# Input fetched transposed in four pieces with the first weights, its squares summed in PSUM, and two weight slices multiplied in native fp32

## The chip, the cores and the metric

The kernel runs on one core of a Trainium2 chip. The metric is the device time of one execution in microseconds (us). Before the change the median of three runs is 904.51 us (904.27 to 905.12).

The engines have these names: PE is TensorE (PEld its weight loads), DVE is VectorE, ACT is ScalarE, POOL is GpSimd, SP is the engine that issues most transfers.

## The reference

One layer on 256 tokens of 1024 channels: a norm, an input projection, three mixers side by side, an output projection with a residual, and a product-key expert layer over 16384 experts.

```python
h = rms_norm(x, norm1_g)              # x: (1, 256, 1024)
proj = h @ w_in                       # 2816 columns
ua, qb, kb, vb, qc, kc, vc, gc = jnp.split(proj, SPLIT_POINTS, axis=-1)
ya = rms_unit(s5_mixer(ua, ...))      # 256 columns: state space, complex phases, a scan over tokens
yb = rms_unit(moba_mixer(qb, kb, vb, ...))            # 8 heads of 64; here one causal block of 256
yc = retention_mixer(qc, kc, vc, gc, ...)             # 4 heads of 64
x = x + (concat(ya, yb, yc) * mix_out_g) @ w_out
x = x + peer_layer(rms_norm(x, norm2_g), w_q, sub_keys, u_emb, v_emb)
```

In `rms_norm` every token is divided by the root of its mean square plus 1e-6 and every channel is multiplied by its gain.

## The kernel before

**Numbers.** Most matmuls are done in halves: an fp32 operand is split into a high part of type fp32r (ScalarE's copy, `w_hi` or `h_hi`) and the rest (`w_lo` or `h_lo`, a subtraction on GpSimd or VectorE). A product of two such operands is three fp32r matmuls, high by high, high by low, low by high (`halves_product`, L438). A native fp32 matmul needs no halves.

**Input projection.** `w_in` comes in six chunks: the s5 input `u` (256 columns, `w_src[0]`) and five of 512 columns, numbered 1 to 5 (q, k and so on). Each chunk lies in one of three slots of `w_ring`, and is cut into eight slices of 128 rows. Slice m (0 to 39) is row block m % 8 of chunk 1 + m // 8. For slice m ScalarE writes `w_hi[:, m % 4]` (`slices_high`, L1399), GpSimd `w_lo[:, m % 4]` (`slices_low`, L1767), and TensorE does six matmuls of 512 columns, three for each half of the tokens (`by_slices`, L464), accumulating over the eight slices in PSUM. The four places of `w_hi` and `w_lo` are used again as `half_used` counts TensorE's slices.

**The front.** The input is loaded by rows into `xs` in two halves of the tokens (L344). TensorE runs eight warming matmuls on zeros (L449), then transposes the input into PSUM banks 0 to 3 (L419). ScalarE squares both halves of the input with the sum over the row as a by-product (L1428). The gained transposed input `hT` (eight chunks of 128 channels by 256 tokens) is written by ScalarE (chunks 0 to 3, `full`, L1459) and VectorE (4 to 7, L892). Chunk `u` is multiplied in native fp32 from `hT` (L459), without the norm's factor; that factor, `rx`, comes from the root on ScalarE (L1397) and a reciprocal on VectorE (L832) and is applied per token when results leave PSUM. The input's high halves are written by ScalarE (0 to 5, `rounded`) and GpSimd (6, 7), the low ones by GpSimd and, for 4 and 5, VectorE.

**The s5 part.** VectorE computes the decay and angle of each state from the parameters (L850 to L878). Phases come from `phase_turns` (a product of time and rate, then two passes that take the whole turns away) and ScalarE's Sin passes `phase_sines`, `phase_sizes`, `phase_cosines`. The second half of the states has its turns from ScalarE (`second_turns`, `second_rounded_up`) and one VectorE pass (L1043), which counts `turn_ready` to 2. TensorE transposes `u` (L519) and the input matrices `bb` (L525), and multiplies them in four drives (`drive(0)` to `drive(3)`, L434). After each drive VectorE runs the complex states (`states(n)`, L986: products, four scans, products).

**What sets the order.** The program is written out by hand, one instruction stream per engine, each strictly in its written order, joined by semaphores. TensorE's order around the change (L515 to L566) interleaves slices with the transposes and drives:

```python
by_slices(1, range(3, KC))
by_slices(2, range(0, 4))
pe.wait_ge(turn_ready, S5_C)      # the second half's turns
drive(1)
by_slices(2, range(4, KC))
turn_heads(0)                     # needs the rotated q of VectorE
by_slices(3, range(0, 6))
pe.wait_ge(states_ready, 2)
drive(2)
```

SP issues the loads in the order of L342 to L366. A slot's next chunk waits until `lo_ready`, GpSimd's count of low halves, shows that the slot is free. The residual is read from `xs` at L1171, after the output projection.

After the projection come the attention and retention scores, the output projection, the queries, and then 128 tiles of expert keys and 128 of values, which fill most of the span; the change touches only their counts on `lo_ready` and `hi_ready`.

## Time and profile before

| | |
|---|---|
| median of 3 runs | 904.51 us |
| profiled execution, its own time | 903.81 us |
| its span | 901.9 us |
| PE busy | 895.0 us (99%) |
| PE weight loads | 780.3 us (87%) |
| DVE busy | 728.9 us (81%) |
| ACT busy | 565.5 us (63%) |
| POOL busy | 426.7 us (47%) |
| DMA | 191.52 MB, mean 212 GB/s |

A row of a timeline gives the start in the span and the duration in us, the line of the code, the operation with what it writes and reads, and in brackets how long the engine was idle before it and what ended that. Matmuls overlap, so the step from one start to the next says more than a matmul's own duration. A native fp32 matmul is recorded as two matmuls.

### The profile page before, as it was taken

The numbers are of one execution on the slowest core, as the hardware profiler recorded it, in microseconds if no ns is written. First come the engines' busy times: TensorE is split into PE (matmuls) and PEld (weight loads), VectorE is DVE, ScalarE is ACT, GpSimd is POOL, SyncE is SP. The second block draws the span as 40 slices with busy tenths as digits, with TensorE's granted clock in tenths as the row PEclk, the third lists the DMA queues.
The fourth block names the chain that finished last, engine by engine and source line by source line (L and its number), as shares of the span: only waits on it lengthen the run. The fifth ranks groups of instructions, "written<-read, shape, count | busy, mean of one in ns | idle before, by whom it ended". The sixth has DMA issues, their size and how long they took to land.

```text
span 901.9 us, 18888 instructions
## 1 busy us (share of the span) xinstructions
PE 895.0 (99%) x5158; PEld 780.3 (87%) x5158; DVE 728.9 (81%) x1659; ACT 565.5 (63%) x1144; POOL 426.7 (47%) x342
## 2 busy tenths in 40 slices
PE   8999999999999999999999999999999999999998
PEld 7777888999999998888888898888888888888886
DVE  7979545299997449999999987888888888888886
ACT  7759566655444567777777776656565655656563
POOL 5875288888888987777777773000000000000000
PEclk9999999999999999999999999999999999999999
DMA  9825050556666665655465557676676766666663
GB/s 337 299 103 187 1 210 24 203 208 231 232 224 224 216 233 188 219 186 218 182 221 183 211 196 258 239 245 237 235 245 242 243 242 243 236 235 247 241 242 128
DMA packets 67755, 191.52 MB, mean 212 GB/s; under 512 B 6672, under 2 KB 8592, under 8 KB 67728
## 3 DMA queue, kind: packets, MB, share of 16 engines
q1 hardware_dynamic: 67440, 191.09, 59.9%
q8 instruction: 14, 0.23, 0.1%
q10 hardware_dynamic: 288, 0.10, 0.0%
q14 instruction: 13, 0.11, 0.0%
HBM read 173.86 MB, written 17.30 MB: 212 GB/s over the span
## 4 chain that ended last, share of the span: by engine, by line
PE 94%; DVE 3%; DMA 1%; ACT 1%; SPq 0%; issue 0%; POOL 0%; DVEq 0%
PE ps L442 20%; PE ps L444 20%; PE ps L443 20%; PE ps L754 16%; PE ps L756 7%; PE ps L764 3%; PE ps L708 1%; PE ps L753 1%; DMA routing<-in_w_in 1%; DVE ps L827 1%; DVE routing L827 1%; PE ps L710 1%; DVE ps L1005 1%; PE ps L727 0%; PE ps L602 0%; PE ps L434 0%
## 5 line engine op out<-in xcount | busy, mean ns | idle before, releaser
L1644 ACT ACTIVATE w_hi<-raw 128x512 fp32r<-128x512 f32 x512 | 308.3, 628 | 135.9 <-PE ps L444 135.1
L1810 POOL TENSOR_TENSOR w_lo<-raw,w_hi 128x512 fp32r<-128x512 f32 x256 | 327.3, 1300 | 69.3 <-ACT w_hi L1644 68.9
L754 PE MATMUL ps<-h_both,w_hi 128*128 128x512 f32 x632 | 225.8, 393 | 0.0
L827 DVE TENSOR_TENSOR w_lo<-raw,w_hi 128x512 fp32r<-128x512 f32 x256 | 177.4, 693 | 57.1 <-ACT w_hi L1644 42.2
L442 PE MATMUL ps<-w_hi,hot_gate 128*128 128x512 f32 x512 | 199.2, 389 | 0.0
L443 PE MATMUL ps<-w_lo,hot_gate 128*128 128x512 f32 x512 | 199.2, 389 | 0.0
L444 PE MATMUL ps<-w_hi,hot_gate 128*128 128x512 f32 x512 | 199.2, 389 | 0.0
L756 PE MATMUL ps<-h_both,w_lo 128*128 128x256 f32 x553 | 154.9, 280 | 0.0
L754 PEld LDWEIGHTS ps<-h_both,w_hi 128*128 128x128 f32 x632 | 117.9, 187 | 20.4
L444 PEld LDWEIGHTS ps<-w_hi,hot_gate 128*128 128x128 f32 x512 | 96.1, 188 | 20.1
L443 PEld LDWEIGHTS ps<-w_lo,hot_gate 128*128 128x128 f32 x512 | 96.1, 188 | 20.0
L442 PEld LDWEIGHTS ps<-w_hi,hot_gate 128*128 128x128 f32 x512 | 96.1, 188 | 19.8
L442 PE MATMUL ps<-h_both,w_hi 128*128 128x256 f32 x392 | 111.1, 284 | 0.0
L1775 POOL TENSOR_TENSOR w_lo<-routing,w_hi 128x512 fp32r<-128x512 f32 x72 | 91.9, 1298 | 40.5 <-ACT w_hi L1411 39.5
L443 PE MATMUL ps<-h_both,w_hi 128*128 128x256 f32 x392 | 110.9, 283 | 0.0
L444 PE MATMUL ps<-h_both,w_lo 128*128 128x256 f32 x392 | 110.9, 283 | 0.0
L1326 DVE SCALAR_TENSOR_TENSOR hot_gate<-ps,route_t 128x256 fp32r<-128x256 f32 x256 | 105.7, 475 | 0.0
L756 PEld LDWEIGHTS ps<-h_both,w_lo 128*128 128x128 f32 x553 | 104.4, 189 | 0.4
L1673 ACT ACTIVATE acts<-ps 128x256 f32<-128x256 f32 x128 | 49.1, 383 | 74.1 <-PE ps L444 66.3
L827 DVE TENSOR_TENSOR route_t<-acts,routing 128x256 f32<-128x256 f32 x128 | 81.6, 637 | 2.5 <-ACT acts L1673 2.0
L443 PEld LDWEIGHTS ps<-h_both,w_hi 128*128 128x128 f32 x392 | 75.2, 192 | 0.2
L442 PEld LDWEIGHTS ps<-h_both,w_hi 128*128 128x128 f32 x392 | 75.2, 192 | 0.1
(242 smaller groups left out, 1236.0 us busy)
## 6 DMA issues: line engine op xcount, KB each, us to landing
raw<-in_u_t SPq DMA_DIRECT2D x128, 512.0 KB, 3.4
raw<-in_v SPq DMA_DIRECT2D x128, 512.0 KB, 3.2
act_spill<-acts SPq DMA_DIRECT2D x62, 256.0 KB, 2.2
acts<-act_spill SPq DMA_DIRECT2D x62, 256.0 KB, 3.4
routing<-in_w_in SPq DMA_DIRECT2D x4, 2048.0 KB, 13.3
routing<-in_w_out SPq DMA_DIRECT2D x2, 2048.0 KB, 8.3
routing<-in_w_q SPq DMA_DIRECT2D x2, 2048.0 KB, 7.6
routing<-in_w_in SPq DMA_DIRECT2D x2, 1024.0 KB, 10.2
```

Source lines behind the costliest of these rows:

```text
L442: pe.matmul(dst, s_hi, m_hi, start=first and i == 0, stop=False)
L443: pe.matmul(dst, s_hi, m_lo, start=False, stop=False)
L444: mm = pe.matmul(dst, s_lo, m_hi, start=False, stop=end)
L754: mm = pe.matmul(ps[:, s % 2, :], s_hi, both, start=(h == 0 and k == 0), stop=end)
L756: mm = pe.matmul(ps[:, s % 2, 0:S], s_lo, m_hi, start=False, stop=False)
L764: mm = pe.matmul(ps[:, 4 + 2 * (s % 2) + q // 2, (q % 2) * 2 * NKEY:(q % 2 + 1) * 2 * NKEY], hot_j[:, s % 2, q, :], hot_gate[:, s % 2, q]. ...
L827: return V.tensor_tensor(out_, a, b, op)
L1326: ins = V.scalar_tensor_tensor(hot_gate[:, s % 2, q], iota_p.unsqueeze(1).to_broadcast([P, 2, NKEY]), route_t[:, 0, one], route_t[:, 2:4, ...
L1644: A.activation(w_hi[:, 2 * (s % 2) + h, :], raw[:, s, h * HALF:(h + 1) * HALF], ACT.Copy)\
L1673: A.activation(acts[:, s, :], ps[:, s % 2, 0:S], ACT.Gelu_apprx_tanh).then_inc(act_ready, 1)
L1775: G.tensor_tensor(w_lo[:, m % 4, :], w_ring[n % W_SLOTS][:, k, :], w_hi[:, m % 4, :].bitcast(F32), ALU.subtract).then_inc(lo_ready, 1)
L1810: G.tensor_tensor(w_lo[:, slot, :], raw[:, s, h * HALF:(h + 1) * HALF], w_hi[:, slot, :].bitcast(F32), ALU.subtract).then_inc(lo_ready, 1)
```

## The change

- The input is also given transposed (`x_t`), and the `u` weights in an order in which a partition's rows lie together (`w_u`). SP loads both in four pieces each, in turn: two chunks of channels of the input (256 KB), two of the weights (256 KB). `xT` lies where the rotation's scratch lies later. The input by rows is loaded later, ahead of the wait for chunk 6 of the weights.
- The transposes of the input go; the warming matmuls are 13 and not 8. The first product waits for a piece of weights every two chunks.
- `hT` is made from `xT` in SBUF, chunks 0 to 3 by ScalarE, 4 to 7 by GpSimd.
- ScalarE squares the four pieces, 512 columns each, the first into PSUM bank 2; VectorE adds them there (five additions), and TensorE sums over the partitions with two one-column fp32 matmuls with a column of ones. ScalarE's root reads that PSUM column.
- Slices 0 and 1 are multiplied in native fp32 from `hT` and the weights; they have no halves, so the counts of `lo_ready` and `hi_ready` are two lower throughout.
- The order on each engine changes: on TensorE the transposes of `u` come after slice 3, those of `bb` after slice 5, the first drive after slice 6, the second after slice 13. On ScalarE the root follows high half 2, and the Sin table the copies of `u`. On VectorE the reciprocal stands inside `phase_turns`, and the low halves of input chunks 0 and 1 after `bb`. On GpSimd the input's halves lie between the slices' low halves.

```diff
+NATIVE = 2
+        xT = rot_tmp.rearrange("p (k t) -> p k t", k=KC)
+        x_sq = qk_flat.rearrange("p (i n) -> p i n", i=4)
+        x_ss, x_part = mv[:, 1, 0:S], mv[:, 1, S:2 * S]
...
             sp.dma_start(vec[:], vecs).then_inc(params_in, 16)
-            for t in range(TT):
-                sp.dma_start(xs[:, t, :], x[t * P:(t + 1) * P, :]).then_inc(x_in[t], 16)
-            first = w_src[0].rearrange("(k p) n -> p k n", p=P)
-            sp.dma_start(w_ring[0][:, 0:4, 0:S5_CH], first[:, 0:4]).then_inc(first_in, 16)
-            sp.dma_start(w_ring[0][:, 4:KC, 0:S5_CH], first[:, 4:KC]).then_inc(w_in_sem[0], 16)
+            for i in range(4):
+                ks = slice(2 * i, 2 * i + 2)
+                sp.dma_start(xT[:, ks], x_t[:, ks]).then_inc(x_t_in[i], 16)
+                sp.dma_start(w_ring[0][:, ks, 0:S5_CH], w_u[:, ks]).then_inc(first_in[i] if i < 3 else w_in_sem[0], 16)
...
                 elif 3 < n <= 8:
-                    sp.wait_ge(lo_ready, KC * (n - W_SLOTS))
+                    if n == 6:
+                        for t in range(TT):
+                            sp.dma_start(xs[:, t, :], x[t * P:(t + 1) * P, :]).then_inc(x_in[t], 16)
+                    sp.wait_ge(lo_ready, KC * (n - W_SLOTS) - NATIVE)
...
-            keep_warm(mv[:, 0, 0:P], 7, 8)
-            pe.wait_ge(con_in, 16)
-            transpose_rows(xs, x_in)
+            keep_warm(mv[:, 0, 0:P], 7, 13)
             for k in range(KC):
-                if k == 0:
-                    pe.wait_ge(first_in, 16)
-                if k == 4:
-                    pe.wait_ge(w_in_sem[0], 16)
-                pe.wait_ge(full_act if k < 4 else full_dve, k % 4 + 1)
+                if k % 2 == 0:
+                    pe.wait_ge(first_in[k // 2] if k < 6 else w_in_sem[0], 16)
+                pe.wait_ge(full_act if k < 4 else full_pool, k % 4 + 1)
...
+            pe.wait_ge(zeros_ready, 6)
+            pe.wait_ge(ss_ready, 1)
+            for t in range(TT):
+                mm = pe.matmul(ps[:, 5, t:t + 1], x_ss[:, t * P:(t + 1) * P], ones, start=True, stop=True)
+            mm.then_inc(ss_psum, 1)
+
+            def native_slices(ks):
+
+                pe.wait_ge(second_in, 16)
+                for k in ks:
+                    for t in range(TT):
+                        mm = pe.matmul(ps[:, t, :], hT[:, k, t * P:(t + 1) * P], w_ring[1][:, k, :], start=(k == 0), stop=False)
+                    mm.then_inc(half_used, 1)
...
-            by_slices(1, range(0, 1))
+            native_slices(range(NATIVE))
+            by_slices(1, range(2, 4))
+            pe.wait_ge(con_in, 16)
             pe.wait_ge(u_tok_ready, TT)
...
-            by_slices(1, range(1, 2))
+            by_slices(1, range(4, 6))
             pe.wait_ge(bb_ready, 1)
...
-            by_slices(1, range(2, 3))
+            by_slices(1, range(6, 7))
             pe.wait_ge(u_ready, 1)
             pe.wait_ge(bT_ready, 1)
             drive(0)
-            by_slices(1, range(3, KC))
-            by_slices(2, range(0, 4))
+            by_slices(1, range(7, KC))
+            by_slices(2, range(0, 6))
             pe.wait_ge(turn_ready, S5_C)
             drive(1)
-            by_slices(2, range(4, KC))
+            by_slices(2, range(6, KC))
...
-            dve.wait_ge(sumsq_x, TT)
-            for k in range(4, KC):
-                dve.wait_ge(t_psum, k // 2 + 1)
-                V.tensor_scalar(hT[:, k, :], ps[:, k // 2, (k % 2) * S:(k % 2 + 1) * S], cols(V_G1 + k, 1), None,
-                                ALU.mult).then_inc(full_dve, 1)
-            dve.wait_ge(full_dve, 4)
+            sq_p = ps[:, 2, :]
+            for i in (1, 2):
+                dve.wait_ge(sq_x, i + 1)
+                step(tt(sq_p, sq_p, x_sq[:, i], ALU.add))
+            dve.wait_ge(sq_x, 4)
+            did(tt(x_part, sq_p[:, 0:S], x_sq[:, 3, 0:S], ALU.add))
+            did(tt(sq_p[:, S:2 * S], sq_p[:, S:2 * S], x_sq[:, 3, S:2 * S], ALU.add))
+            settle()
+            tt(x_ss, sq_p[:, S:2 * S], x_part, ALU.add).then_inc(ss_ready, 1)
+            dve.wait_ge(ss_ready, 1)
...
                 step(tt(turns, now, rate, ALU.mult))
+                rstd_of(1, 0, TT, rx[:, 0:TT]).then_inc(rx_ready, 1)
...
             phase_turns(0, 2, phi)
-            rstd_of(1, 0, TT, rx[:, 0:TT]).then_inc(rx_ready, 1)
-            for k in (4, 5):
-                dve.wait_ge(th_ready, k + 1)
-                tt(h_lo[:, k, :], hT[:, k, :], h_hi[:, k, :].bitcast(F32), ALU.subtract).then_inc(tl_first, 1)
...
+            def squares_x(i):
+
+                act.wait_ge(x_t_in[i], 16)
+                A.activation(ps[:, 2, :] if i == 0 else x_sq[:, i], xT[:, 2 * i:2 * i + 2].rearrange("p k t -> p (k t)"),
+                             ACT.Square).then_inc(sq_x, 1)
...
+            act.wait_ge(zeros_ready, 5)
+            A.activation(spare, quarter, ACT.Exp)
             act.wait_ge(params_in, 16)
             for k in range(4):
                 full(k)
...
+                if k == 1:
+                    squares_x(0)
+                    act.wait_ge(expo_ready, 1)
+                    A.activation(mag, expo, ACT.Exp).then_inc(mag_ready, 1)
+            squares_x(1)
+            squares_x(2)
+            rounded((2, 3))
+            squares_x(3)
+            rounded((0, 1))
+            A.activation(spare, quarter, ACT.Sqrt)
+            slices_high(range(2, 3))
+            act.wait_ge(ss_psum, 1)
+            root(ps[:, 5, 0:TT], 0, 1.0 / D)
+            slices_high(range(3, 4))
...
+            act.wait_ge(ang_ready, 1)
+            did(A.activation(s1, ang, ACT.Sin))
+            settle()
+            A.activation(c1, half, ACT.Sin).then_inc(trig_ready, 1)
+            rounded((6, 7))
+            slices_high(range(4, 5))
             phase_sines(0)
-            slices_high(range(2, 3))
+            slices_high(range(5, 6))
...
+            pool.wait_ge(params_in, 16)
+            for k in range(4, KC):
+                pool.wait_ge(x_t_in[k // 2], 16)
+                G.tensor_tensor(hT[:, k, :], xT[:, k, :], cols(V_G1 + k, 1).to_broadcast([P, S]), ALU.mult).then_inc(full_pool, 1)
...
+            for k in (2, 3):
+                pool.wait_ge(th_ready, k - 1)
+                input_low(k)
+            input_halves(4)
+            slices_low(range(2, 4))
+            input_halves(5)
+            slices_low(range(4, 6))
             for k in (6, 7):
...
                 input_low(k)
-                slices_low(range(k - 5, k - 4))
-            slices_low(range(3, 33))
+                slices_low(range(k, k + 1))
+            slices_low(range(8, 33))
```

## Rows read from the trace of the kernel before

**Rows 1.** shares of the last chain by engine (page, fourth part).

```profile
PE 94%; DVE 3%; DMA 1%; ACT 1%; SPq 0%; issue 0%; POOL 0%; DVEq 0%
```

**Rows 2.** busy time by stretch and engine; then clock, DMA share, GB/s.

```profile
20.40:42.30 21.90, 21.90 (x103) 17.15 (x103) 19.89 (x37) 17.59 (x28) 19.42 (x16) 1.00 0.82 293
42.30:55.70 13.40, 13.40 (x67) 10.51 (x66) 8.25 (x19) 9.58 (x15) 10.36 (x9) 1.00 0.44 152
```

**Rows 3.** the last chain in order of time: start us, us, what.

```profile
23.11 0.43 PE ps L442
...
24.69 0.24 PE ps L442
...
26.07 0.23 PE ps L442
...
55.59 0.23 PE ps L442
...
66.81 1.30 DVE routing L1086 x2
```

**Rows 4.** timeline of VectorE: start us, us, operation [idle before, releaser].

```profile
10.80 1.56 DVE L827 TENSOR_TENSOR ps<-con,small 128x1024 f32<-128x1024 f32 x1
...
23.25 1.29 DVE L827 TENSOR_TENSOR route_t<-ps,routing 128x512 f32<-128x512 f32 x2 [1.42 <-PE ps L434]
...
32.48 1.22 DVE L1043 SCALAR_TENSOR_TENSOR routing<-routing,ps 128x1024 f32<-128x1024 f32 x1
...
36.94 1.29 DVE L827 TENSOR_TENSOR route_t<-ps,routing 128x512 f32<-128x512 f32 x2
...
55.73 0.48 DVE L954 SCALAR_TENSOR_TENSOR routing<-ps,small,raw 128x256 f32<-128x256 f32 x1 [2.97 <-PE ps L444]
```

**Rows 5.** timeline of TensorE; an fp32 matmul is two records.

```profile
8.65 7.17 PE L459 MATMUL ps<-routing 128*128 128x256 f32 x32 [0.67 <-DMA routing<-in_w_in]
15.48 0.58 PE L442 MATMUL ps<-w_hi,h_both 128*128 128x512 f32 x1
...
19.79 0.66 PE L525 MATMUL ps<-con,raw 128*128 128x128 f32 x4
...
21.97 1.13 PE L434 MATMUL ps<-routing,raw 32*128 32x256 f32 x8
```

**Rows 6.** warming matmuls by line: ns min/median/max, first and last start.

```profile
L427 PE MATMUL ps<-routing x16: 421/421/582, 1.1 to 4.4; 128*128 128x128 f32 x16
```

**Rows 7.** three DMA lines of SP, each with time from issue to landing.

```profile
L344 SPq DMA_DIRECT2D xs<-in_x x2: 422/423/424, 1.2 to 1.7; - x2
...
DMA to landing us min/median/max: 3.7/4.4/5.2
...
L346 SPq DMA_DIRECT2D routing<-in_w_in x1: 433/433/433, 2.1 to 2.1; - x1
...
DMA to landing us min/median/max: 6.5/6.5/6.5
...
L350 SPq DMA_DIRECT2D routing<-in_w_in x1: 448/448/448, 4.0 to 4.0; - x1
...
DMA to landing us min/median/max: 9.2/9.2/9.2
```

**Rows 8.** timeline of ScalarE.

```profile
6.23 0.21 ACT L1508 ACTIVATE small<-small 128x8 f32<-128x8 f32 x1 [0.20 <-DVE small L827]
...
7.93 1.54 ACT L1462 ACTIVATE routing<-ps,vec 128x256 f32<-128x256 f32 x4
...
13.87 1.28 ACT L1519 ACT_TABLE_LOAD   x1
...
34.80 1.04 ACT L1446 ACTIVATE routing<-routing 128x1024 f32<-128x1024 f32 x1
```

**Rows 9.** GpSimd's low parts of the input and of the slices.

```profile
L1787 POOL TENSOR_TENSOR h_both<-routing,h_both x6: 725/735/1710, 9.9 to 18.3; 128x256 fp32r<-128x256 f32 x6
...
L1775 POOL TENSOR_TENSOR w_lo<-routing,w_hi x29: 1265/1291/1306, 13.9 to 59.6; 128x512 fp32r<-128x512 f32 x29
```

111 lines of the change are left out of this document (44 added, 67 removed).

## The prediction

> **What bounds the kernel now.** I read the page first. The last chain is 94% TensorE [rows 1], so only what TensorE waits for, or does in addition, can move the end. The change touches the front of the program, so I then read the stretches one by one: from 20.4 to 42.3 us TensorE is busy without a gap, and VectorE for 19.9 of 21.9 us beside it, while from 42.3 to 55.7 it has 5 us to spare [rows 2]. The chain shows the unit to count in. A slice of a projection (six fp32r matmuls) takes 1.38 us (24.69 to 26.07), and the first slice after another kind of work 1.58 us (23.11 to 24.69). The slice numbered 24 (first of chunk 4) starts at 55.59, and at 66.81 the chain passes to VectorE, behind scores of TensorE at a fixed place in that order [rows 3]. From slice 24 on nothing in the change alters the order of work, VectorE starts its key rotation there behind a TensorE slice after 2.97 us of idleness [rows 4], and the passage at 66.81 follows. So the question is when slice 24 starts afterwards, and whether VectorE is still on time there.
>
> **The front, step by step.** *Start of the first product.* Now it starts at 8.65 and has 32 passes in 6.83 us (8.65 to the next work at 15.48), 0.2135 us a pass of 256 columns [rows 5], which is 2.4 GHz. The 16 transposes before it go. The 13 warming matmuls are 26 passes; the present 16 start from 1.1 to 4.4 [rows 6], 0.22 us each for 128 columns, which is 1.2 GHz. At that pace 26 end at 1.06 + 26 x 0.22 = 6.8. Input and weights: the halves of the input (512 KB each) are issued at 1.2 and 1.7 and landed 3.7 and 5.2 us later (4.9 and 6.9), the first weights issued at 2.1 landed at 8.6 [rows 7]. So 0.5, 1.0, 1.5 MB are there at 4.9, 6.9, 8.6. The new order is piece of input, piece of weights, 0.25 MB each: first pair at 4.9, second 6.9, third 8.6, fourth, with 1.7 us more, 10.3. ScalarE scales a 256-column chunk in 0.385 us [rows 8]: chunks 0 and 1 done by 5.0; 2 and 3 stand behind the exponential, which starts at 6.23 now [rows 8] as its operand comes from an untouched VectorE chain; they end by 7.2, and TensorE wants them at 8.5. GpSimd scales chunks 4 to 7: such an operation took 0.735 us, its very first 1.71 [rows 9]. From 7.7 (half way between the landings 6.9 and 8.6, the third input piece) chunk 7 is ready at 7.7 + 1.71 + 3 x 0.735 = 11.6, wanted at 6.8 + 28 x 0.2135 = 12.8. So the product runs 6.8 to 13.6: 1.85 us gained.
>
> *Sums of squares.* Four passes of one column with a weight load each; no such row is there. Below, the bound is 0; above, four passes of 256 columns, 0.85. The four 128-column transposes at 19.79 took 0.66 with their change of work [rows 5], and that is nearest: 0.55, to 14.2. VectorE's five additions, about 2.6 us by its 512-column operations (1.29 us for two [rows 4]), start when its parameter chain ends, near 9.1 to 9.4, and end by 12: hidden under the product.
>
> *Two slices in fp32.* Four matmuls of 512 columns are 8 passes of twice 0.2135 = 3.42 us, in place of 2 x 1.37. That costs 0.68 us; they need no halves. Their weights land at 4.0 + 9.2 = 13.2 now [rows 7]. SP issues more pieces before them (eight of 0.43 us for four), so they go out at 5.5 and not 4.0, but the bytes ahead of them are the same and keep the queue full beyond 7 us. I leave 13.2; the other end is 14.7, the issue's whole delay. Native slices: 14.2 to 17.7. Below nothing the swap can't go, as even the nearest rows give TensorE more columns.
>
> *What the squares' new path delays.* Today VectorE's phase product starts at 10.80 [rows 4]; the root of the sums now waits for TensorE's sums (14.3), behind the high half that follows the landing of the second weights. Root 14.6, reciprocal 14.8, and only then the two passes of the phases, 1.22 us each as the one at 32.48 [rows 4]: turns ready at 17.3. ScalarE then brings the Sin table after the copies of u, not before (1.28 us [rows 8]), to 17.2. From the end of that load (13.87 + 1.28) to the transposes of b at 19.79 go 4.6 us today [rows 5, 8], so b is ready at 21.8. TensorE wants their transposes only at 24.2, see below, so this lateness is covered.
>
> *TensorE to the first drive.* From 17.7: slices 2 and 3 (1.58 + 1.38) 20.7; transposes of u 0.6, 21.3; slices 4 and 5, 24.2; transposes of b 0.66, 24.9; slice 6. ScalarE copies u at 21.4, then the sizes (1 us), then high half 6 by 23.5; GpSimd's low half takes 1.29 us [rows 9]: 24.8, just in time. Slice 6 ends at 26.5, the first drive at 27.55 (1.06 us; now it starts at 21.97 [rows 5]). GpSimd itself: four multiplications to 11.6, two low parts to 13.1, one pair of halves (1.2) to 14.3, low halves 2 and 3 to 16.9, halves 5 to 18.1, low halves 4 and 5, paced by ScalarE's high halves (18.8, 20.2), to 20.1 and 21.6: each before TensorE wants it.
>
> *The second drive.* It waits for the second phase turns, which VectorE makes after its first states. Now states start at 23.25, 0.15 us after the first drive, and the turns are ready at 32.48 + 1.22 = 33.7 [rows 4]: 10.6 us behind the drive. Between the drives stand nine slices today, over 12.3 us, so no wait, and afterwards seven: 1.58 + 6 x 1.38 = 9.8. TensorE reaches the second drive at 37.3, the turns come at 27.55 + 10.6 = 38.15, and it ends at 39.3. That is a wait of 0.8 to 0.9 us that isn't there today. Queued behind TensorE's wait are slices 14 and 15; and ScalarE's second sines (34.80 now, without idle time [rows 8]) wait for the same turns, with high half 15 behind them: 38.2 + 1.0 + 0.6, GpSimd's low half to 41.15. Slice 14 ends at 40.9, so slice 15 waits 0.3: 41.2 to 42.6.
>
> *To slice 24.* Transposes of q 0.9 (rotated q is ready 3.25 us after the turns, 33.7 to 36.94 today [rows 4]: 41.4), 43.5; slices 16 to 21, 51.7 (ScalarE's head copy, projection and squares end at 46.9, high half 20 47.4, low half 48.75, wanted at 48.97); the third drive wants states 1, as long as states 0 (23.25 to 32.48): 9.2 us from 41.5 = 50.7, and ends at 52.8; slices 22, 23: 55.7. VectorE's sums, ScalarE's Sqrt table and root, and the normalised k end at 55.35, VectorE's next wait ends about 56: it has 0.7 us of its 2.97 left.
>
> **The sum.** Slice 24 at 55.7 for 55.59: 0.1 later. In terms: 1.85 at the start, about 0.9 from waits of today that go (0.36 and 0.2 around slice 1, and slice 0 to 2's switches, which fall among fewer slices) against 0.55, 0.68, 0.85, 0.3 and some 0.2 to 0.3 of small waits. The input by rows is loaded again behind the fifth weights, in a stretch (42.3 to 55.7) in which the queues move 152 GB/s, about half of the 293 of the stretch before [rows 2], and is read by nothing before the output projection's sum: nothing. The profiled execution of now took 903.81 (span 901.9), so 903.9 by the sum, and against the median of 904.51 it is 904.6; the terms are not good to 0.1, and I forecast 904.5, no change. Own range: 903.5 to 905.5. Changes under 0.2% (1.8 us, 902.7 to 906.3) count as none.
>
> **Two places where the skill speaks.** The present warming passes run at 1.2 GHz until 4.4 [rows 6] and the product's at 2.4 from 8.65 [rows 5]. The Trainium skill, "TensorE: Matmul & The Clock Gate", Part 1: The HAM clock gate, says that the moment at which the clock rises is not tied to the program's start and differs from run to run. By that rule the unbroken warming could see 2.4 GHz before 6.8; the rival on the clock below says what that gives. The input's 512 KB pieces landed 2.0 and 1.7 us apart [rows 7]. The skill's "DMA: Bandwidth & Descriptors", section Bandwidth, advises transfers of 1 MiB and more, as small ones get less of the rate; that speaks against eight pieces of 256 KB. By it the later pieces and the second weights would land late, the 14.7 end above; the pieces overlap in the queue, so I keep to the rows.
>
> **Rivals.** (a) *The gain stays.* If the low halves and the turns come in time, by VectorE's states or ScalarE's passes going quicker beside fewer neighbours, the waits of 0.85 + 0.3 + 0.1 vanish: 904.6 - 1.25 = 903.3. Against it: 10.6 us behind the drive is read from rows, and 9.8 is counted. Chance 0.15. (b) *The clock rises early.* If at 4.6, 10 of 26 passes go at half the time, the product starts at 5.8, but its fourth piece lands at 10.3 and the second weights at 13.2: the native slices can start 1.0 earlier, and all behind them: 903.5; with (a), 902.3. Chance 0.15, of both 0.12 more. (c) *Slower: GpSimd gates the first product.* Chunks 4 to 7 multiply by a column held for 256 elements, a form that today's GpSimd rows lack. Decisive from 1.0 us each ((12.8 - 7.7 - 1.0)/4). At the 1.29 us of its 512-column form [rows 9] chunk 7 is ready at 13.9, the product ends 1.1 later: 905.7; at twice 0.735, 14.6: 1.8 later, and with the second weights at 14.7, 906.8. Chance 0.13. (d) *It does less than it says*: the second weights land at 14.7, the root and native slices 0.5 to 1.0 late: 905.4. Chance 0.10. The forecast holds 0.35.
>
> Beyond 1.8 us faster: the joint case and a part of (a) and (b), 0.20. Beyond 1.8 slower: half of (c) and a little of (d) and of a late VectorE at 56 (which has 0.7 us left), 0.12. Else 0.68. The range, 902.3 to 906.3, reaches to the joint case and the middle of (c).
>
> **What would show it.** Right: the first product starts at 6.6 to 7.0; native matmuls take 3.4 us from 14.2; TensorE idles 0.6 to 1.1 us before the second drive, released by VectorE's turns; slice 24 within 0.7 us of 55.6. Wrong: a first product that waits for GpSimd, second weights beyond 14, a second drive without a wait, or VectorE late at the key rotation, which then sets the chain.

## The result and the profile after

The changed kernel takes 905.36 us (median of 22 runs, 904.51 to 907.40) where the kernel before takes 904.14 in the same session (22 runs, 903.21 to 905.57). The ratio is 1.0015, 95% interval 1.0009 to 1.0021: 1.2 us slower, small but outside what chance gives. The forecast was 904.5 and no change. A second series of the very same kernel (run 1 below) gave 905.32 against 904.07. Three executions far off the rest (1102.63 us in run 11, 1804.01 and 3815.34 us of the kernel before beside runs 1 to 4) explain nothing here and hardly move a median.

The profiled execution of the changed kernel is one of its fastest, 904.51 us with a span of 902.7 (before: 903.81 and 901.9), so it shows 0.7 us in its time and 0.8 in its span; the second run's profile (905.07, span 903.3) is nearer to the median, and both are read below. Line numbers after differ: L452 is the first product, L460 the sums, L468 the native slices, L439 to L441 the three parts of a slice, L431 the drives, L1056 the second turns.

TensorE's timeline of the kernel after, its front (start us, us, operation, [idle before, releaser]), answers to [rows 5 and 6]:

```profile
1.06 4.78 PE L424 MATMUL ps<-routing 128*128 128x128 f32 x26 [1.06 <-DVE small L847]
6.13 7.60 PE L452 MATMUL ps<-routing 128*128 128x256 f32 x32 [0.29 <-DMA routing<-in_w_u]
13.57 0.50 PE L460 MATMUL ps<-small,routing 128*128 128x1 f32 x4
...
26.35 1.13 PE L431 MATMUL ps<-routing,raw 32*128 32x256 f32 x8
```

```profile
38.14 1.13 PE L431 MATMUL ps<-routing,raw 32*128 32x256 f32 x8 [0.93 <-DVE routing L1056]
...
41.13 0.50 PE L439 MATMUL ps<-w_hi,h_both 128*128 128x512 f32 x1 [0.27 <-POOL w_lo L1795]
...
42.63 1.04 PE L504 MATMUL ps<-con,routing 128*128 128x128 f32 x8
```

The first product starts at 6.13 (8.65 before). The native slices' first matmul, at 14.29, is in the chain below behind a transfer. The second drive has a wait of 0.93 us in front, ended by VectorE's second turns; slice 15 waits 0.27 for GpSimd; the transposes of q follow at 42.63, where they stood at 42.17 before.

The last chain of the kernel after, in order of time (start us, us, what), answers to [rows 3]:

```profile
6.20 8.05 DMA routing<-in_w_in
...
14.29 3.70 PE ps L468 x8
17.99 0.23 PE ps L439
...
23.37 1.29 POOL w_lo L1795
...
26.42 1.09 PE ps L431 x8
...
27.63 1.30 DVE route_t L835 x2
...
36.86 1.23 DVE routing L1056
...
38.15 0.94 issue
...
39.77 1.31 POOL w_lo L1795
...
41.13 0.50 PE ps L439
```

```profile
56.06 0.23 PE ps L439
...
67.29 1.30 DVE routing L1099 x2
```

Before the change the chain ran on TensorE alone in this stretch. Now it begins with the landing of the second weights (issue at 6.20, 8.05 us), goes through the native slices, a ScalarE and a GpSimd pass (slice 6), the first drive, all of VectorE's first states to the turns (27.63 to 38.1), then a pass of GpSimd. Slice 24 starts at 56.06, not 55.59, and the chain passes to VectorE at 67.29, not 66.81: 0.47 later each.

The same two stretches as in [rows 2], of the kernel after (us, busy time of TensorE, its weight loads, VectorE, ScalarE and GpSimd with their instructions, clock, DMA share, GB/s):

```profile
20.40:42.30 21.90, 20.29 (x97) 15.38 (x96) 19.29 (x36) 16.99 (x28) 16.80 (x15) 1.00 0.77 280
42.30:55.70 13.40, 13.40 (x67) 10.44 (x66) 12.48 (x25) 10.17 (x16) 11.89 (x11) 1.00 0.76 272
```

TensorE works 20.29 of the 21.90 us that it filled before: the 1.6 us missing are the waits above and the one at slice 6. The second stretch moves 272 GB/s in place of 152, the input loaded again, and costs TensorE nothing: 13.40 of 13.40.

The rest of the 0.8 us of span sits later, between the two groups of four mixed-output transposes. The chain of the kernel after there, and under it the copy in question in ScalarE's timeline of the kernel before and of the one after:

```profile
124.28 0.24 PE ps L441
...
124.57 0.33 issue
124.89 0.47 ACT h_both L1434
```

```profile
124.13 0.47 ACT L1420 ACTIVATE h_both<-ps,vec 128x256 fp32r<-128x256 f32 x1 [0.67 <-PE ps L444]
```

```profile
124.89 0.47 ACT L1434 ACTIVATE h_both<-ps,vec 128x256 fp32r<-128x256 f32 x1 [0.95 <-PE ps L441]
```

TensorE's part ends at 124.5, and ScalarE's last copy back begins only at 124.89: it sat idle 0.95 us before it, against 0.67 before. The two groups of transposes start 9.62 us apart after (122.10 and 131.72) and 9.34 before (121.61 and 130.95). That is 0.28 us at a place that no line of the change touches. From the second group to the end of the span the two profiles agree: 771.0 us after (902.7 - 131.7), 770.95 before.

### The profile page after: what moved, and what is told of

Read it like the earlier page. It is cut to its first block, busy times and chain, and to the rows that moved or that the text cites. A ratio compares the mean times of both kernels' runs of the same rounds, so it can differ in the third digit from the quotient of the medians.

```text
span 902.7 us, 18892 instructions
## 1 busy us (share of the span) xinstructions
PE 895.1 (99%) x5152; PEld 778.7 (86%) x5152; DVE 731.2 (81%) x1661; ACT 563.3 (62%) x1144; POOL 426.4 (47%) x344
## 4 chain that ended last, share of the span: by engine, by line
PE 92%; DVE 4%; DMA 1%; ACT 1%; POOL 1%; SPq 1%; issue 0%; DVEq 0%; ACTq 0%
PE ps L439 20%; PE ps L440 19%; PE ps L441 19%; PE ps L762 16%; PE ps L764 7%; PE ps L772 3%; PE ps L716 1%; PE ps L761 1%; DVE routing L835 1%; DVE ps L835 1%; DMA routing<-in_w_in 1%; DVE ps L1018 1%; PE ps L718 1%; POOL w_lo L1795 1%; PE ps L735 0%; DVE route_t L835 0%
## 5 line engine op out<-in xcount | busy, mean ns | idle before, releaser
L439 PE MATMUL ps<-w_hi,hot_gate 128*128 128x512 f32 x512 | 199.2, 389 | 0.0
L441 PE MATMUL ps<-w_hi,hot_gate 128*128 128x512 f32 x512 | 199.2, 389 | 0.0
L439 PEld LDWEIGHTS ps<-w_hi,hot_gate 128*128 128x128 f32 x512 | 96.1, 188 | 20.1
L441 PEld LDWEIGHTS ps<-w_hi,hot_gate 128*128 128x128 f32 x512 | 96.1, 188 | 19.9
L439 PE MATMUL ps<-h_both,w_hi 128*128 128x256 f32 x392 | 111.1, 284 | 0.0
L441 PE MATMUL ps<-h_both,w_lo 128*128 128x256 f32 x392 | 110.9, 283 | 0.0
L1795 POOL TENSOR_TENSOR w_lo<-routing,w_hi 128x512 fp32r<-128x512 f32 x70 | 89.5, 1302 | 41.8 <-ACT w_hi L1425 41.0
L439 PEld LDWEIGHTS ps<-h_both,w_hi 128*128 128x128 f32 x392 | 75.1, 192 | 0.1
```

The lines of the kernel that those rows point to most:

```text
L439: pe.matmul(dst, s_hi, m_hi, start=first and i == 0, stop=False)
L441: mm = pe.matmul(dst, s_lo, m_hi, start=False, stop=end)
L1795: G.tensor_tensor(w_lo[:, m % 4, :], w_ring[n % W_SLOTS][:, k, :], w_hi[:, m % 4, :].bitcast(F32), ALU.subtract).then_inc(lo_ready, 1)
```

## The experiments

Fifteen runs of kernels on the chip, each with executions of the kernel before beside it; ratios are to that, and not exactly the quotient of the two medians. Runs 1 to 4 share one chip, 5 to 8, 9 to 12 and 13 to 15 one each; the kernel before has medians of 904.07, 904.63, 903.98 and 904.08 on them, so runs are best compared within a group. "Distance of the drives" is from the start of the first drive to that of the second on TensorE: 11.79 us in the profile after.

**1. The changed kernel again.** No edit.

> The changed kernel again, unchanged, as the base of this series. The theory of waits (TensorE's wait for the second phase turns, and second weights that land a microsecond late) expects 1.2 us over the kernel before, ratio 1.0013, with slice 24 at 56.1 and a second drive that waits 0.9 us. The rival, that the slowdown is a chance of single runs (landing times, moment of the clock's rise), expects slice 24 within 0.2 us of the kernel before's 55.6 in a second trace and a ratio whose interval holds 1.000.

905.32 us (12 runs), 1.0019 (1.0011 to 1.0028). Its profile, TensorE first and then VectorE; then VectorE of the first profile after, and of before:

```profile
6.29 1.89 PE L452 MATMUL ps<-routing 128*128 128x256 f32 x8
8.77 5.45 PE L452 MATMUL ps<-routing 128*128 128x256 f32 x24 [0.58 <-DMA routing<-in_w_u]
...
26.78 1.13 PE L431 MATMUL ps<-routing,raw 32*128 32x256 f32 x8
...
38.86 1.13 PE L431 MATMUL ps<-routing,raw 32*128 32x256 f32 x8 [1.19 <-DVE routing L1056]
```

```profile
24.85 0.69 DVE L960 COPY raw<-ps 128x512 f32<-128x512 f32 x1 [1.24 <-PE ps L533]
25.46 2.85 DVE L835 TENSOR_TENSOR raw<-raw,vec 128x32 f32<-128x32 f32 x3
28.34 1.29 DVE L835 TENSOR_TENSOR route_t<-ps,routing 128x512 f32<-128x512 f32 x2
```

```profile
24.42 0.69 DVE L960 COPY raw<-ps 128x512 f32<-128x512 f32 x1 [1.24 <-PE ps L533]
25.03 1.68 DVE L835 TENSOR_TENSOR raw<-raw,vec 128x32 f32<-128x32 f32 x3
27.63 1.29 DVE L835 TENSOR_TENSOR route_t<-ps,routing 128x512 f32<-128x512 f32 x2 [0.92 <-PE ps L431]
```

```profile
21.09 0.75 DVE L827 TENSOR_TENSOR raw<-raw,vec 128x32 f32<-128x32 f32 x3
```

Three things differ from the profile above. The product waits 0.58 us within itself for a piece of the first weights. The second weights (issued 6.1, 8.6 to landing) are there at 14.7 and the native slices start at 14.73. And three tiny VectorE operations, which scale the rotation of k (128x32 elements each), took 2.85 us here, 1.68 in the first profile after and 0.75 before. Here they end at 28.31, 0.4 after the first drive, and the states start at 28.34 without idle time: 1.56 us after the drive's start, where the other profile has 1.28. The distance of the drives is 12.08 for 11.79, the wait 1.19 for 0.93.

**2. The second turns earlier.** VectorE makes them between the products and the scans of the first states.

```diff
-            states(0)
-            dve.wait_ge(rounded_up, 1)
-            V.scalar_tensor_tensor(pair(zb[:, 4:8]), ...)
+            states(0, second_phase_turns)     # called ahead of the four scans
```

> VectorE makes the second half's phase turns between the products and the scans of its first states, not after them. Theory of waits: the turns come 4.9 us earlier (near 33 us), the second drive doesn't wait (0.93 us now) and slice 15 doesn't either (0.27), slice 24 starts near 55.0, and VectorE, whose other work ends no sooner, is late by 0.2 to 0.3 at the key rotation: about 1.0 us faster than the changed kernel, near the time of the kernel before or 0.2 over it. Rival, VectorE's chain of states sets this stretch and the wait only shows it: no gain over the changed kernel, the wait moves to the transposes of q or the third drive.

904.47 us, 1.0003 (0.9994 to 1.0012), not to be told from the kernel before: 0.85 us of the loss comes back against run 1 on the same chip. A part of this is the clock: three of run 1's twelve executions show a mean granted clock of 0.998 and take 906.22 to 907.26, none of run 2's does (more on this at the end). Without them it is 905.10 against 904.47, so 0.63 of the 1.25 us over the kernel before (903.85 by the same count). The second drive has no wait and starts at 37.97. In exchange the first states end later: the transposes of q wait 0.25 at 42.30 and the late scores 0.26 at 60.69 for VectorE. So the wait for the turns was at least half of the loss, and VectorE has little room to pay with.

**3. The input in two pieces.** As before the change, but transposed: pieces of 512 KB of input and weights.

```diff
-            for i in range(4):
-                ks = slice(2 * i, 2 * i + 2)
+            for i in range(2):
+                ks = slice(4 * i, 4 * i + 4)
```

> Input and first weights come in two pieces each, in turn (512 KB), not in four. If the issues of the eight pieces made the second weights late (they go out at 6.2 us and not 4.0), they go out 1.9 us sooner and land near 13.2, not 14.25, and the first product, which starts at 6.13 now, starts near 6.9 with its first 512 KB of weights: the native slices start near 13.9, 0.4 us sooner, and the time is 0.3 us lower. Rival, the queue is full anyway and only bytes count: the second weights still land near 14.2, the product starts 0.8 later and ends near 14: the time is equal or up to 0.3 us higher.

905.47 us, 1.0017 (1.0008 to 1.0026). The second weights' issue moved from 6.2 to 3.9, but they landed 9.6 later, at 13.5. The first product started 1 us later (7.25, after 0.92 of waiting for the weights) and the sums at 14.27. Both ends of the trade cancel: fewer pieces don't repair the front. (The waits of the engines follow the two pieces; that part of the diff isn't shown.)

**4. The second weights' rows in two transfers.** Slice 0 waits for its own rows only.

```diff
-            sp.dma_start(w_ring[1][:, 0:4], second[:, 0:4]).then_inc(second_in, 16)
+            sp.dma_start(w_ring[1][:, 0:2], second[:, 0:2]).then_inc(second_in, 16)
+            sp.dma_start(w_ring[1][:, 2:4], second[:, 2:4]).then_inc(third_in, 16)
```

> The first half of the second weights (1 MB) comes in two loads, and the native slices wait for the first 512 KB only. Theory of waits: it lands about 1.2 us before 14.25, the native slices start at 13.95 when the sums are done (0.3 us sooner), and everything up to the first drive moves with it as long as ScalarE and GpSimd keep up; but the high half 2 waits for the second load, and the second drive's wait for the turns remains as it counts from the first drive: 0.3 us lower at most. Rival, GpSimd's low halves pace slices 4 to 6 (slice 6 waits 0.41 us for one): nothing is gained, time equal within 0.1 us.

905.08 us, 1.0012 (1.0003 to 1.0020). The native slices (14.79) follow the sums (14.43) without a wait. About 0.2 us of the loss, not resolved by the intervals.

**5. The second drive one slice later**, after slice 14.

> TensorE's second drive stands after slice 14, not after slice 13; all else as in the changed kernel. The chain of waits puts the loss on turns (VectorE, near 38), second sines (ScalarE), high half 15, low half 15 (GpSimd, ready near 41.1), slice 15. By that theory the idle time only moves: no wait of 0.93 us before the drive, 1.2 us or so before slice 15 in its place, time equal to the changed kernel within 0.2 us. Rival, TensorE's own wait at the drive is the loss: 0.9 us faster than the changed kernel.

905.47 us for 904.63 (1.0012, 1.0003 to 1.0021). The drive (38.48) doesn't wait, and slice 15 then waits 1.72 for GpSimd at 41.34. The wait only moves: ScalarE's second sines stand in front of the high half of slice 15 and want the same turns. TensorE's place for the drive isn't the limit, VectorE's chain from the first drive to the turns is. In this profile (905.97 us) the granted clock also fell to 0.50, 1.2 GHz, for 3.42 us from within that wait on (start:end, us, busy time of TensorE, its weight loads, VectorE, ScalarE and GpSimd, clock, DMA share, GB/s):

```profile
40.97:44.39 3.42, 3.06 (x8) 2.37 (x9) 3.25 (x8) 2.60 (x5) 2.95 (x4) 0.50 0.50 152
```

The six matmuls of slice 15 go from 41.34 to 44.06, 2.72 us, where the profile after has 1.50. Four of the eleven executions show a mean clock of 0.998; the median of the other seven is 905.31, so the verdict stays.

**6. The two slices as six fp32r matmuls again**, with the halves they need and, for these, another order of the input's halves on ScalarE and GpSimd; TensorE's order is kept.

> Slices 0 and 1 are again done in halves: ScalarE writes their high parts, GpSimd their low parts and the low parts of input chunks 0 and 1 (VectorE's two are gone); the order on TensorE is else that of the changed kernel. If the native slices are the loss (3.7 us measured for what takes 2.75 in halves), this is 0.9 us faster than the changed kernel. Theory: they are what makes the early start of use, since halves can't be ready: high half 0 at 15, low half 0 at 16.3, and GpSimd's chain (four more operations, 1.3 us each for the slices, 0.7 for the input) then sets slices 0 to 6: the first drive 2 to 3.5 us later, the time 2 to 3.5 us higher than the changed kernel's.

910.99 us (5 runs), 1.0064 (1.0051 to 1.0078). Slice 0 waits 2.44 us for GpSimd at 17.22, the first drive starts at 30.87 and the second waits 2.40 at 44.17. The native slices cost TensorE about 0.6 us: from their start to the transposes of u (14.29 to 20.60 in the profile after) go 6.31 us, of which slices 2 and 3 are 1.58 + 1.38, which leaves 3.35 for 2 x 1.38. Without them the kernel is 5.5 us slower than run 5 on the same chip. Not all of this is waiting: the clock is at 0.50 from 17.09 to 20.50 and from 44.40 to 51.22 in this profile (913.13 us), around the two long waits. The two executions at a mean clock of 0.999 or more took 909.75 and 910.13, against 905.31 of run 5 by the same count, and that is still 4.4 to 4.8 us. The native slices are not the loss: they cover the halves that come late.

**7. The first drive one slice earlier.** The transposes of b after slice 4, the drive after slice 5.

```diff
-            by_slices(1, range(4, 6))
+            by_slices(1, range(4, 5))
...
-            by_slices(1, range(6, 7))
+            by_slices(1, range(5, 6))
...
-            by_slices(1, range(7, KC))
+            by_slices(1, range(6, KC))
```

> The transposes of b stand after slice 4 (not 5), the first drive after slice 5 (not 6). Theory: the first drive, and with it VectorE's states and the second turns, were put back further than their inputs need; b is ready at 21.9 and TensorE waits 0.4 us before slice 6 for a low half. The first drive then ends near 25.5 and not 27.5, the turns come near 36.1, TensorE reaches the second drive at 36.7 without a wait, the transposes of q start near 40.7 and not 42.6: 1.4 to 1.9 us faster than the changed kernel, 0.2 to 0.7 us faster than the kernel before. Rival, the landing of the second weights and GpSimd's low halves set this stretch: 0.4 us faster at most.

903.42 us for 904.63, 0.9988 (0.9979 to 0.9997). The first drive starts at 24.91, the second at 37.62 without a wait, the third at 50.89. One place in TensorE's order turns the loss into a gain. On this chip the kernel before has a mean clock of 0.998 in 11 of 27 executions, run 7 in none; the other 16 have a median of 904.31, so the gain is 0.9 us rather than 1.2.

**8. Edits 7 and 4 together.**

> The first drive earlier, as in the run before, and the first half of the second weights in two loads, of which the native slices wait for the first only. Theory of waits: the split takes another 0.2 to 0.4 us (it took 0.2 when alone, with the drives unchanged), together 1.7 to 2.2 us under the changed kernel and 0.5 to 1.0 under the kernel before. Rival, the first product, whose last piece and whose input chunks by GpSimd come at 11 to 12 us, ends at 14.3 in such runs and sets the native slices whatever the weights do: equal to the run before within 0.1 us.

902.98 us for 904.63, 0.9981 (0.9972 to 0.9990). TensorE and then VectorE in the profile of 8:

```profile
14.02 0.50 PE L462 MATMUL ps<-small,routing 128*128 128x1 f32 x4
14.38 3.68 PE L470 MATMUL ps<-routing 128*128 128x512 f32 x8
...
24.67 1.13 PE L433 MATMUL ps<-routing,raw 32*128 32x256 f32 x8
...
37.15 1.13 PE L433 MATMUL ps<-routing,raw 32*128 32x256 f32 x8
```

```profile
22.39 1.36 DVE L837 TENSOR_TENSOR h_both<-routing,h_both 128x256 fp32r<-128x256 f32 x2
...
24.28 1.39 DVE L837 TENSOR_TENSOR raw<-raw,vec 128x32 f32<-128x32 f32 x3
25.95 1.29 DVE L837 TENSOR_TENSOR route_t<-ps,routing 128x512 f32<-128x512 f32 x2 [0.28 <-PE ps L433]
```

The three tiny operations end before the drive does, since VectorE still idles 0.28 us for it.

**9. The three tiny operations at 9 us.** They are issued with those for q.

```diff
             for a, b in ((0, half_rope), (half_rope, 0)):
                 did(tt(rope_q[:, 1, :, a:a + half_rope], ...))
+            did(tt(rope_k[:, 0], rope[:, 0], ...))
+            for a, b in ((0, half_rope), (half_rope, 0)):
+                did(tt(rope_k[:, 1, :, a:a + half_rope], ...))
             settle()
...
-            did(tt(rope_k[:, 0], rope[:, 0], ...))   # and the two after it, ahead of states(0)
```

> The kernel after, with one edit: the three 128x32 VectorE operations that prepare the key rotation are issued with the three like them for the query rotation, at about 9 us, rather than between the copy of the transposed b matrices and the first state pair. Theory (small operations beside GpSimd): they took 0.75 us in the kernel before, 1.68 in the profile of the changed kernel and 2.85 in its second profile, where they end at 28.31, so the first state pair starts 1.56 us after the first drive rather than 1.28. Moved, they take about 0.4 us at 9 us, in VectorE's idle time before the sums of squares (0.66 and 0.26 idle there); the state pair starts 1.28 after the drive in every run, the second drive 11.79 after the first, and the median falls by 0.2 to 0.4 us against the changed kernel: 905.0 where that shows 905.3, ratio to before about 1.0010. Rival (they are slow but hidden in most runs; the typical run is slow for another reason): the second drive's distance from the first stays at 12.05 and the ratio at 1.0015 to 1.0019.

904.92 us for 903.98, 1.0010 (1.0001 to 1.0018). VectorE in the profile of 9:

```profile
8.52 0.63 DVE L835 TENSOR_TENSOR raw<-raw,vec 128x32 f32<-128x32 f32 x6
...
24.98 0.69 DVE L965 COPY raw<-ps 128x512 f32<-128x512 f32 x1 [1.09 <-PE ps L533]
28.16 1.29 DVE L835 TENSOR_TENSOR route_t<-ps,routing 128x512 f32<-128x512 f32 x2 [2.49 <-PE ps L431]
```

All six took 0.63 us there, where three took 2.85 beside GpSimd. VectorE idles 2.49 us for the drive, the states start 1.25 after it (26.91), and the distance of the drives is 11.76. In the time the gain, 0.4 us against run 1, lies within the intervals.

**10. Two tiny copies more on ScalarE** at about 61 us, where it has 2.96 us idle.

```diff
             heads_back(1, mkT, cols(V_HEAD, 1))
+            for i in range(2):
+                A.activation(pads[:, i:i + 1], quarter, ACT.Copy)
```

> The kernel after with two tiny ScalarE copies more (128x1 to places that nothing reads), issued at about 61 us where ScalarE is idle for 2.96. Theory (ScalarE's late start at 124.9 us depends on where the instruction stands in its program): the kernel before and the one with two more weight slices on ScalarE need 9.34 and 9.36 us from the first to the second four mixed-output transposes, every variant with the native slices 9.61 or 9.62, and in those ScalarE begins the fourth copy back 0.95 us after it was free rather than 0.67. With two instructions more ahead of it the distance is 9.34 and the time falls by 0.28 us: ratio to before 1.0012 where the changed kernel has 1.0015. Rival (it is a matter of what else runs in those microseconds, or of the native slices): the distance stays 9.61 and the time with it, or the late start shows up at another ScalarE instruction on the chain and nothing is gained.

```profile
125.26 0.48 ACT L1435 ACTIVATE h_both<-ps,vec 128x256 fp32r<-128x256 f32 x1 [0.68 <-PE ps L442]
```

```profile
122.74 1.03 PE L684 MATMUL ps<-con,xs 128*128 128x128 f32 x8
...
132.09 1.09 PE L684 MATMUL ps<-con,xs 128*128 128x128 f32 x8
```

These are ScalarE's last copy and TensorE's two groups of transposes in the profile of 10. Two operations that compute nothing took the late start away: 0.68 idle, and the transposes are 9.35 us apart. The time, 905.13 us, 1.0015 (1.0006 to 1.0024), is no lower for it. Its 11 executions go from 904.55 to 907.29, which would hide 0.27 us; but there is more to it than scatter. The time of an execution is longer than its span, by 1.81 to 1.86 us in the mean of each of the eleven series without the two copies (or run 6's two high halves), and by 2.12 to 2.13 in runs 10, 12 and 6, as in 13 and 14 below; for the kernel before it is 1.95. So what the two instructions took out of the span came back outside it.

**11 and 12. Version 8 with the tiny operations at 9 us; and with the two copies too.**

> The combined version (first drive one slice earlier, second weights' rows in two transfers) with the key rotation's three small VectorE operations moved to about 9 us. In that version's profile the state pair waited 0.28 us for the drive after they had ended, so they were hidden. Theory: only the runs in which they take over 1.6 us gain, 0 to 0.2 us: 902.9 where that version shows 903.0, ratio 0.9980. Rival (they delay the sums of squares at 9 us, and with them the start of the states): 0.1 to 0.3 us slower than that version, ratio 0.9984.

> The same with the two ScalarE pads as well. If the late start depends on the position, 0.28 us less than without the pads: ratio 0.9977, 9.34 us between the transposes. If not, no difference.

903.48 us, 0.9989 (0.9980 to 0.9998), and 903.56, 0.9993 (0.9984 to 1.0002), both for 903.98. The edit that helped in 9 gained nothing in the median here. VectorE, GpSimd, the same of 8 beside it, and TensorE in the profile of 12:

```profile
22.61 2.45 DVE L838 TENSOR_TENSOR h_both<-routing,h_both 128x256 fp32r<-128x256 f32 x2
24.98 0.68 DVE L968 COPY raw<-ps 128x512 f32<-128x512 f32 x1
```

```profile
22.55 0.74 POOL L1811 TENSOR_TENSOR h_both<-routing,h_both 128x256 fp32r<-128x256 f32 x1
23.48 1.30 POOL L1799 TENSOR_TENSOR w_lo<-routing,w_hi 128x512 fp32r<-128x512 f32 x1 [0.18 <-ACT w_hi L1427]
```

and GpSimd in the profile of 8:

```profile
22.55 0.92 POOL L1809 TENSOR_TENSOR h_both<-routing,h_both 128x256 fp32r<-128x256 f32 x1
```

```profile
25.81 1.13 PE L434 MATMUL ps<-routing,raw 32*128 32x256 f32 x8 [1.01 <-DVE raw L968]
```

VectorE's two subtractions for halves of the input (both operands in SBUF, as in the tiny three) took 2.45 us in place of 1.36. The single ones were 0.96 and 1.56 us long, the first starting at 22.61 just behind GpSimd's at 22.55, the second at 23.5 just behind GpSimd's at 23.48. In version 8 the first started ahead of GpSimd's (22.39 for 22.55) and took 0.48, and there it was GpSimd's that took longer, 0.92 for 0.74. The copy of b's transposes then ended at 25.7, and TensorE waited 1.01 us for it in front of the first drive, at 25.81 rather than 24.67. With the operations at 9 us VectorE came 0.2 us later (8.2 us behind the native slices' start for 8.0) and into GpSimd's way. This needn't happen in every execution: of run 11's executions five took 902.44 to 902.63, under the fastest of version 8 (902.64), and six 903.47 to 904.49, about 1 us more, and both profiles (904.49 and 903.70) are of the slower kind. That the faster kind lacks the wait fits, but there is no trace of one.

**13. Version 8 with the two copies only, 14. the changed kernel with 9 and 10, 15. version 8 again**, on one chip.

> The first drive one slice earlier, the second weights' rows in two transfers, and the two ScalarE pads; the key rotation's operations where the changed kernel has them. Theory: moved to 9 us, those three made VectorE arrive 0.27 later at its two subtractions of input halves (both operands in SBUF), which then met GpSimd's subtractions and took 2.40 and 2.45 us for 1.36, so that the first drive waited about 1.0 us for VectorE. Left in place, the subtractions take 1.36 and the drive doesn't wait; with the pads the time is 0.28 below that version without them: ratio 0.9978 where that shows 0.9981. Rival (the time of the combined version was luck of its chip): both show 0.999, as the versions with the operations moved did.

> The kernel after with both repairs, the key rotation's operations at 9 us and the two ScalarE pads, and nothing of the rest. If the two effects add, 0.25 and 0.27 us come off: ratio 1.0007 to 1.0010, second drive 11.8 after the first and 9.35 between the mixed-output transposes. If only one counts in the time, 1.0012.

> The combined version without pads again, beside the same runs of before, so that the pads are weighed on one chip. Theory: 0.9981 again. Rival: 0.999.

Against 904.08 (27 runs) they took 903.14, 0.9989 (0.9980 to 0.9998); 905.22, 1.0014 (1.0005 to 1.0024); and 902.89, 0.9989 (0.9980 to 0.9998). Version 8's own time repeats within 0.1 us on another chip (902.98, 902.89), while the kernel before was 904.63 on the one and 904.08 on the other, so the gain is 1.2 to 1.6 us by all executions; without those of the kernel before at a mean clock of 0.998 (904.31 and 904.06) it is 1.3 and 1.2. With the operations left in place VectorE's subtractions took 1.37 in version 13, as expected, and the drive didn't wait (24.89). The two copies brought 9.35 us between the transposes in 13 and 9.33 in 14, yet no time in the medians (+0.25 for version 13 against 15): the median span of 13 is 901.0 for 901.1 in 15, and its time is longer than the span by 2.12 us, for 1.82. And 14 has both repairs in its trace, drives 11.76 and transposes 9.33 apart, with a span of 902.6 at its fastest, and its median is still 905.22: that the two effects add up to 0.5 us of the median is refuted.

## Why the prediction was wrong, step by step

In the fastest execution the mechanism came as forecast up to 42.6 us. The sum was too low by an addition of mine behind that, by a late start on ScalarE, and, in a typical execution, by the landing of the second weights and by VectorE's way from the first drive to the turns. The median of 905.36 lies in my own range of 903.5 to 905.5 by luck: the range was laid around the 904.51 of three executions, and the kernel before turned out at 904.14 over 22. First the profiled execution, then the median.

- *Start of the product:* 6.8 forecast, 6.13 measured, 6.09 to 6.77 in the other profiles with four pieces. The clock half of rival (b) happened in some (after: warming passes 0.21 us apart up to 4.4 us, 0.11 from there on), and was worth nothing, as the first weights' pieces or GpSimd's first chunk then gated the product: from its start to the sums it took 7.44 us, and 7.76 in run 1, for 6.83 before, and the sums of run 5, which started at 6.77, come at 13.72 all the same. The sums start at 13.57 and 14.05, forecast 13.6.
- *Third piece of the input:* I had it at 7.7. GpSimd's first multiplication, which waits for it, starts at 9.28, and between 9.18 (run 5) and 10.45 (run 11) in the other profiles with four pieces. Its four took 2.47 us and not 3.9, the first no longer than the rest, so the last ends at 11.7 and not at 11.6. The 1.71 us that I took from [rows 9] for GpSimd's first operation belong to its third (11.23 to 12.94), which began while VectorE's 1.56 us operation of [rows 4] ran; its first took 0.72. The late piece and this misread price cancelled. Rival (c) was right in its place and wrong in its price: TensorE waits for GpSimd in the product of runs 4, 6, 7, 9, 11 and 12, by 0.22 to 0.55 us. Its 906.8 was too high by my own numbers: a product that ends 1.8 us later ends behind weights that land at 14.7, so these add nothing to 906.4.
- *Second weights:* I took the landing of before, 13.2; they land at 14.25 (issue 6.20 + 8.05), and at 14.7 in run 1. They go out at 6.20 and not at the 5.5 that I had, as the input's pieces took 0.47 us each to issue and the last of the weights 1.02. Issued 2.2 us later, they land 1.05 to 1.5 later. Because the sums end at 14.1, the native slices still start at 14.29, forecast 14.2; but in run 1 at 14.73 and in run 2's profile at 15.11. This is rival (d), to which I gave 0.10. Its 905.4 is what the median became, but by more terms than its own, as shown below.
- *Native slices:* 3.42 forecast. The 3.70 of the profile holds the last matmul's own duration; by the starts it is about 3.35 (14.29 to the transposes of u at 20.60, less 1.58 + 1.38), so this term was right to 0.1.
- *Slice 6:* I had its low half just in time; TensorE came 0.4 earlier than forecast and waits 0.41 for it.
- *First drive:* its end 27.55 forecast, 27.51 measured. *Turns:* 38.15 and 38.1. *Second drive's wait:* 0.8 to 0.9 and 0.93. *Slice 15:* 0.3 and 0.27. *Transposes of q:* 42.6 and 42.63.
- *From there to slice 24, the step that failed in this execution:* "transposes of q 0.9, slices 16 to 21, 51.7 ... 55.7" is 13.1 us. The profile before has 13.42 from 42.17 to 55.59 and the profile after 13.43 from 42.63 to 56.06. With 1.58 + 5 x 1.38 = 8.5 for the six slices, 43.5 becomes 52.0, not 51.7: the third drive starts at 51.98. I added 0.3 us too little, in a stretch that doesn't change at all, and the +0.4 that the steps said became +0.1. The terms listed after the sum didn't catch it: 1.85 + 0.9 against 0.55 + 0.68 + 0.85 + 0.3 + 0.2 to 0.3 is 0.1 earlier, and not the 0.1 later of the steps.
- *Behind slice 24:* VectorE's slack at the key rotation, 0.7 forecast, is 1.02, and 67.29 is 0.47 late like slice 24, as forecast. But the late start of ScalarE at 124.9 adds 0.28, where the text had "nothing alters the order, so the passage follows". Together 0.75 of the 0.8 us between the two profiles.

For the median: the typical execution of the changed kernel is 0.85 us behind its fastest (905.36 and 904.51), that of the kernel before 0.3 us behind its profiled one. Run 1's profile, at 905.07, is 1.26 us over the profiled execution before, as the medians are 1.22 apart, so its rows show the typical loss term by term against my steps:

- *Second weights kept at 13.2:* they land at 14.7, the native slices start at 14.73 for 14.2, and the first drive ends about 27.9 for 27.55. That is 0.35 us, and about 0.2 of it is what run 4 brought back, within its interval.
- *10.6 us from the drive to the turns:* here it is 10.9, as the three tiny operations beside GpSimd push the first states back; no step of mine had them. I carried the 0.15 us from the drive's end to the states over from [rows 4] without asking what VectorE does ahead of it. With this the transposes of q stand at 43.34 for 42.6.
- *The addition to slice 24:* 56.79 for 55.7, another 0.3 us.
- *The late start on ScalarE:* 0.28 us, put at nothing.

With the +0.1 of the sum that makes 1.4 to 1.5 us, and the two spans are 1.4 us apart (903.3 and 901.9). The time is less far apart because the changed kernel's time exceeds its span by 1.84 us and that of the kernel before by 1.95.

What can be had back is shown by the runs: the wait for VectorE's turns. Runs 2, 7 and 8 take it away and are 0.9, 1.9 and 2.4 us faster than the changed kernel (905.36; 7 and 8 on another chip than run 1), and run 5 shows that it can't be dodged on TensorE alone. The forecast knew of this wait and its size. Of the 2.5 us gained at the start (8.65 to 6.13), 1.2 are left where the native slices start (14.29, for slice 0 at 15.48 before) and 1.2 at slice 7 (27.41 for 28.62); the waits of 0.93 and 0.27 us, with the changes of work around them, spend this and 0.46 more up to the transposes of q.

What stays open: the parts don't add up in the medians. Run 14 repairs in its trace both the tiny operations' place and the late start, and is still at 905.22 (span 902.6 at its fastest). For the late start the longer time outside the span answers this, for the tiny operations nothing does. That the late start at 124.9 depends on where the instruction stands in ScalarE's program is supported by runs 6 (two high halves more on ScalarE, 9.36 us) and 10, 12, 13 and 14 (two copies more, 9.33 to 9.36), against the eleven profiles without (9.61 or 9.62); what in the chip makes it so, and why the time outside the span moves the other way, no run tells.

## What to carry to other kernels

When TensorE's front gets shorter, count its distance to the first result that another engine makes from it: with a fixed chain of 10.6 us on VectorE behind the first drive, removing TensorE's own waits mostly turns them into one wait for that chain, and the repair is to place the first drive a slice earlier, not to feed TensorE faster. A transfer whose issue is pushed back by small pieces lands later even when the bytes ahead of it are the same: take the later end of its bounds. And a stretch that a change leaves alone should be taken as one length from the trace (13.42 us here), not added up again from its parts. A gain read inside the span should be looked for in the time as well: 0.27 us between two points of the trace was worth nothing outside.
